# ScalarE's order inside one head of two softmax attentions: all four exponentials, then the copies

## The chip, the cores and the metric

The kernel is one program on one core of a Trainium2 chip. The metric is the device time of one execution in microseconds (us), the median over several. One core has five engines that run independently and meet only at semaphores: TensorE (PE, with its weight loads as PEld), VectorE (DVE), ScalarE (ACT), GpSimd (POOL) and SyncE (SP, which issues transfers). Each works through its own list of instructions in order.

## The reference

Two model blocks run one after the other on 512 positions of width 1024. Two attentions in the second block matter here: a sparse one with 8 heads of width 64, in which each query sees at most 128 chosen keys, and a latent one with 16 heads of width 64 + 32.

```python
# layer 0: 8 heads, keys chosen per query (here a mask added to the logits does the choosing)
logits = jnp.einsum('bqhd,bqkhd->bhqk', qb, k_sel).astype(jnp.float32) * (dh ** -0.5)
logits = jnp.where(valid[:, None], logits, -jnp.inf)
p = jax.nn.softmax(logits, axis=-1).astype(v.dtype)
return jnp.einsum('bhqk,bqkhd->bqhd', p, v_sel).reshape(bsz, Q_BLOCK, h * dh)
...
# layer 1: 16 heads, causal
logits = (jnp.einsum('bqhd,bshd->bhqs', qnb, k_nope)
          + jnp.einsum('bqhr,bsr->bhqs', qrb, k_rope)).astype(jnp.float32) * scale
p = jax.nn.softmax(logits, axis=-1).astype(v.dtype)
return jnp.einsum('bhqs,bshd->bqhd', p, v).reshape(bsz, Q_BLOCK, C_HEADS * C_V_DIM)
```

Each of them is followed by an output product, norms and a squared-ReLU MLP.

## The kernel before

A head has four blocks of 128 queries. Query block t sees 128(t+1) keys, so one head has logits of 512, 384, 128 and 256 columns for t = 3, 2, 0, 1. They lie in three banks of PSUM. Even heads use the tile PM, odd heads the tile PDT (PX[n % 2] in the code), so two heads are in the works at once. The last bank (index 3) of each tile serves other products.

A head n passes through the engines like this:

1. TensorE, `logits(n)` (L1558): eight groups of products for the four query blocks, written to PX[n % 2]. Ahead of them it waits in `probs_taken` for both copies of head n-2, which lay in the same banks.
2. VectorE, `row_least(n)` (L3162): adds the mask, takes the least of each row (the logits carry a minus sign), and raises att_max once for each of the four blocks.
3. ScalarE, `exps(n)` (L2297): four exponentials, each followed by a read of the row sum.
4. TensorE, `turn_probs(n)` (L1576): ten 128x128 transposes, back into the same banks. It waits for all four exponentials.
5. ScalarE, `turned(n)` (L2304), copies the first bank (512 columns) of the turned probabilities out, and VectorE, also `turned(n)` (L3169), the other two (768 columns). Only then are the banks free for head n+2.
6. TensorE, `pair_values` (L1597): the products with the values, for two heads together, in two halves; every second head also turns the row sums (`turn_den`, L1584).

The loops are software-pipelined by hand. In step h TensorE does logits(h), then (latent attention only) `turn_q(h + 2)` (L1684), which turns the query of a later head, then turn_probs(h-1), then values. In step h ScalarE does exps(h) and turned(h-1), in the latent attention also `turned_q(h + 2)` (L2369), a copy of the turned query. TensorE's wait is

```python
def probs_taken(n):
    pe.wait_ge(S("probs_s"), n)
    pe.wait_ge(S("probs_v"), n)
```

where probs_s is raised by ScalarE's copy and probs_v by VectorE's; logits(h) is preceded by probs_taken(h-1), that is by the copies of head h-2. `turn_q(h + 2)` waits for tr_read, which ScalarE raises with turned_q(h+1): all turned queries from head 1 on pass through one bank, PDT bank 3.

Of the kernel before, what the change touches and what calls it, by code (L numbers as in the profile page):

```python
# [51 lines left out]
A_H = 8  # L52
TOPK = 128
C_H = 16
# [113 lines left out]
def build_program(nc, x, c, w_ada, b_ada, norm_in_gain, w_in, conv_w, conv_b, dt_bias, a_log, d_skip,  # L168
# [15 lines left out]
    def S(name):  # L184
        if name not in sems:
            sems[name] = ctx.enter_context(nc.semaphore(name))
        return sems[name]
# [60 lines left out]
    def arena(name, shape, kb, dtype=F32):  # L248
        return at(name, shape, dtype, offset=A0 + int(kb * KB))
# [66 lines left out]
    pr = [arena("pr0", [P, 1280], 8), arena("pr1", [P, 1280], 13)]  # L316
# [3 lines left out]
    mx = arena("mx", [P, 4, TT], 77.625)  # L320
    den = arena("den", [P, 4, TT], 77.75)
# [29 lines left out]
    pr3 = [arena("pr30", [P, 1280], 9), arena("pr31", [P, 1280], 16)]  # L351
# [4 lines left out]
    mx3 = arena("mx3", [P, 4, TT], 26)  # L356
    den3 = arena("den3", [P, 4, TT], 26.5)
# [95 lines left out]
    def full_wait(eng, name, b, r, unit):  # L453

        if b < 3:
            eng.wait_ge(S(f"bank_full{b}"), r + (PH[name][2][b] + 1))
        else:
            eng.wait_ge(S("w_used"), unit + 1)
# [61 lines left out]
    def head_group(h):  # L520

        return TR["heads"][0] + 1 + h + max(0, (h - 4) // 2)
# [1233 lines left out]
    def _(act):  # L1756
# [363 lines left out]
        def after_piece(name, r, h, b):  # L2120

            u = PH[name][0] + 2 * r + h
            if (b == last_bank(name, r, h) or name == "dt") and (name, r, h) not in (("wout_a", 1, 1), ("z_attn", 0, 1), ("qk2", 1, 1),
                                                               ("gates", 2, 1)):
                hi(0, u + 2, 0)
            if h == 1 and name != "z_attn":
                full_wait(act, name, b, r, u)
                if name == "gates":
                    dst = gb[:, b, :]
                elif name == "xbc":  # L2130
                    dst = xbc[:, 4 * r + b, 3:SEQ + 3]
                else:
                    dst = {"z_ssm": zs, "wout_a": mix, "qk2": qk_tm}[name][:, b, 512 * r:512 * r + 512]
                scale = rstd[:, 1, b:b + 1] if name == "wout_a" else 1.0
                nc.scalar.activation(dst, PD[b], ACT.Copy, scale=scale).then_inc(S(f"bank_free{b}"), 1)
# [145 lines left out]
        def convolution2_high(f):  # L2281
            act.wait_ge(S("w_used"), PH["wo2"][0])
            act.wait_ge(S("conv2_out"), f + 1)
            nc.scalar.activation(hhi[:, 4 + f, :], ca[:, f, :], ACT.Copy).then_inc(S("conv2_hi"), 1)

        def exps(n, p, m, d, order):

            s = n % 2
            if n >= 2:
                act.wait_ge(S("att_turned"), n - 1)  # L2290
            if n >= 4:
                act.wait_ge(S("den_wide"), n - 3)
            for q, t in order:
                b, c0 = QB_AT[t]
                w = (t + 1) * P
                act.wait_ge(S("att_max"), 4 * n + (1, 3, 3, 4)[q])
                nc.scalar.activation(p[s][:, QB_FIRST[t]:QB_FIRST[t] + w], PX[s][:, b, c0:c0 + w], ACT.Exp, scale=-1.0,  # L2297
                                     bias=m[:, n % 4, t:t + 1], accum_out=d[:, n % 4, t:t + 1]).then_inc(S("att_exps"), 1)

        def turned(n, pt):  # L2300
            act.wait_ge(S("att_turned"), n + 1)
            if n >= 4:
                act.wait_ge(S("att_pv"), n // 2 - 1)
            nc.scalar.activation(pt[n % 4][:, 0:SEQ], PX[n % 2][:, 0, :], ACT.Copy).then_inc(S("probs_s"), 1)  # L2304

        def turned_den(pair):

            act.wait_ge(S("tr_done"), den_group(pair) + 1)
            if pair >= 2:
                act.wait_ge(S("attn_low"), KT + pair - 1)  # L2310
            nc.scalar.activation(lat[pair % 2][:, :], den_bank(pair), ACT.Copy).then_inc(S("tr_read"), 1)

        def lat_high(pair, k):

            act.wait_ge(S("att_out"), pair + 1)
            nc.scalar.activation(hhi[:, k, :], lat[pair % 2][:, :], ACT.Copy).then_inc(S("attn_high"), 1)

        for h in range(A_H + 4):
            if h < A_H:
                exps(h, pr, mx, den, ((0, 3), (1, 2)))  # L2320
            if 1 <= h <= A_H:
                turned(h - 1, prt)
            if h < A_H:
                exps(h, pr, mx, den, ((2, 0), (3, 1)))
            if h == 2:
                after_piece(*GATE_PIECES[7])
            if 3 <= h < 7:
                convolution2_high(h - 3)
            if h >= 5 and h % 2:
                lat_high((h - 5) // 2, (h - 5) // 2)  # L2330
            if h >= 3 and h % 2 and h < A_H + 3:
                turned_den((h - 3) // 2)
# [33 lines left out]
        def turned_q(h):  # L2366
            act.wait_ge(S("tr_done"), head_group(h) + 1)
            X = PDT if h else PM
            nc.scalar.activation(qth[h % 2][0:C_QK, :], X[0:C_QK, 3, :], ACT.Copy, scale=-C_QK ** -0.5)\  # L2369
                .then_inc(S("tr_read"), 1)  # L2370
# [23 lines left out]
        for h in range(C_H + 4):  # L2394
            n = A_H + h
            if h < C_H:
                exps(n, pr3, mx3, den3, ((0, 3), (1, 2)))
            if h + 2 < C_H:
                turned_q(h + 2)
            if h == 3:  # L2400
                act.wait_ge(S("w_used"), PH["wo3"][0])
            if 1 <= h <= C_H:
                turned(n - 1, prt3)
            if h < C_H:
                exps(n, pr3, mx3, den3, ((2, 0), (3, 1)))
            if h in (1, 2):
                full_wait(act, "ukv", h + 1, 3, u0 + 1)
                nc.scalar.activation(v3[:, h + 1, 512:DM], PM[:, 3, :], ACT.Copy).then_inc(S(f"bank_free{h + 1}"), 1)
            if h >= 5 and h % 2:
                lat_high((n - 5) // 2, (h - 5) // 2)  # L2410
            if h >= 3 and h % 2 and h < C_H + 3:
                turned_den((n - 3) // 2)
# [180 lines left out]
    def _(dve):  # L2593
# [776 lines left out]
        def ends(name):  # L3370
# [13 lines left out]
            def fifth(_):  # L3384

                m = mixm[:, 2:4, 512:DM]
                v.tensor_tensor(m, m, PDT[:, 2:4, :], ALU.subtract).then_inc(S("mlp_sum"), 1)

            def seventh(_):

                dve.wait_ge(S("w_used"), u + turn_of(3, P7) + 1)
                dve.wait_ge(S("mlp_sum"), made + 7)
                m = mixm[:, 2:4, 512:DM]
                v.tensor_tensor(m, m, PDT[:, 0:2, :], ALU.subtract).then_inc(S("mlp_sum"), 1)
                m = mixm[:, 2:4, 0:512]
                v.tensor_tensor(m, m, PDT[:, 0:2, :], ALU.add).then_inc(S("mlp_sum"), 1)

            def last_lo(_):

                dve.wait_ge(S("w_hi"), u + P4 + 1)  # L3400
                raw, w = wraw[RAW[u + P4][0]], (u + P4) % 2
                v.tensor_tensor(wlo[w][:, :], raw[:, :], fl(whi[w][:, :]), ALU.subtract).then_inc(S("w_split"), 1)
# [91 lines left out]
```

## Time and profile before

| | |
|---|---|
| median of 3 runs | 1733.22 us |
| lowest and highest | 1733.17, 1734.76 us |
| the profiled execution | 1732.95 us, of which the span of the profile 1731.1 us |
| granted TensorE clock, mean over the span | 0.998 |
| busy share of the span | PE 98%, DVE 63%, ACT 52%, POOL 22% |
| the sparse attention (8 heads) | about 759 to 795 us in the span |
| the latent attention (16 heads) | about 1256 to 1343 us in the span |

A row of a timeline has the start in us, the duration in us, the engine, the line, the operation, output<-inputs, the sizes, and how many instructions it merges; in brackets the idle time of the engine ahead of it and what ended that. A duration beside neighbours that start before it has ended is normal: instructions of one engine overlap a little.

### The profile page before, as it was taken

What the parts mean: (1) busy time and instruction counts of PE and PEld (TensorE: products, weight loads), DVE (VectorE), ACT (ScalarE), POOL (GpSimd) and SP (SyncE); (2) the same over time, 40 slices, a digit from 0 to 9 for tenths busy, and PEclk for the clock granted to TensorE, in tenths of its full rate; (3) what the DMA queues carried; (4) which work ended last, traced back from release to release, by engine and by line L of the source; (5) the groups of instructions that cost most, each with busy time, mean ns of one, the idle gap of its engine ahead of it and who ended that gap; (6) DMA issues with size and microseconds to landing.
All of it is one profiled execution on the core that took longest, in us unless ns stands there. A gap on an engine that the chain in (4) does not pass through costs nothing.

```text
span 1731.1 us, 21441 instructions
## 1 busy us (share of the span) xinstructions
PE 1695.2 (98%) x8391; PEld 1364.7 (79%) x8391; DVE 1097.2 (63%) x1449; ACT 896.7 (52%) x1428; POOL 377.2 (22%) x226
## 2 busy tenths in 40 slices
PE   7999999999999999999999999998999999999997
PEld 5898777778787867877988888888866798888886
DVE  6786567685976367953455565595457246565488
ACT  4435656556635353255564535456677356353553
POOL 0200232123244233433400100105410340010100
PEclk9999999999999999999999999999999999999999
DMA  8632322222132322223377775782310247775695
GB/s 318 231 121 75 97 63 65 71 73 72 51 122 81 98 73 72 96 77 110 108 182 187 161 199 145 171 192 83 104 60 1 97 153 164 195 157 184 146 218 135
DMA packets 109377, 216.62 MB, mean 125 GB/s; under 512 B 6905, under 2 KB 9086, under 8 KB 109278
## 3 DMA queue, kind: packets, MB, share of 16 engines
q1 hardware_dynamic: 89214, 175.42, 30.8%
q0 software_dynamic: 20064, 39.85, 13.7%
q8 instruction: 66, 1.08, 0.3%
q14 instruction: 33, 0.27, 0.0%
HBM read 205.88 MB, written 2.10 MB: 120 GB/s over the span
## 4 chain that ended last, share of the span: by engine, by line
PE 88%; DVE 7%; ACT 2%; issue 2%; DMA 1%; POOL 0%; SPq 0%; DVEq 0%; ACTq 0%
PE PDT L873 9%; PE PDT L875 9%; PE PDT L874 9%; PE PDT L862 6%; PE PDT L864 6%; PE PDT L863 6%; PE PM L1070 5%; PE PM L1063 5%; PE PM L1065 5%; PE PM L1321 2%; PE PM L1597 2%; PE PM L1288 1%; PE PM L1558 1%; PE PDT L1558 1%; PE PM L1349 1%
## 5 line engine op out<-in xcount | busy, mean ns | idle before, releaser
L2442 POOL TENSOR_TENSOR wlo<-wraw,whi 128x512 fp32r<-128x512 f32 (+5 forms) x103 | 284.4, 2779 | 570.0 <-ACT whi L1771 398.6
L3217 DVE TENSOR_TENSOR wlo<-wraw,whi 128x2048 fp32r<-128x2048 f32 x82 | 187.9, 2292 | 197.1 <-ACT whi L1889 196.9
L1889 ACT ACTIVATE whi<-wraw 128x2048 fp32r<-128x2048 f32 x82 | 157.1, 1916 | 260.8 <-PE PM L1070 131.8
L873 PE MATMUL PDT<-hhi,whi 128*128 128x512 f32 x732 | 287.4, 393 | 1.1 <-POOL wlo L2442 1.1
L875 PE MATMUL PDT<-hhi,wlo 128*128 128x512 f32 x732 | 285.2, 390 | 0.0
L874 PE MATMUL PDT<-hlo,whi 128*128 128x512 f32 x732 | 285.2, 390 | 0.0
L862 PE MATMUL PDT<-whi,hhi 128*128 128x512 f32 (+1 forms) x528 | 208.0, 394 | 1.1 <-DVE hlo L2951 0.6
L864 PE MATMUL PDT<-whi,hlo 128*128 128x512 f32 (+1 forms) x528 | 202.9, 384 | 0.0
L863 PE MATMUL PDT<-wlo,hhi 128*128 128x512 f32 (+1 forms) x528 | 202.9, 384 | 0.0
L1771 ACT ACTIVATE whi<-wraw 128x2048 fp32r<-128x2048 f32 (+4 forms) x63 | 113.9, 1808 | 131.4 <-PE PDT L864 59.9
L2568 POOL DMA_DIRECT2D wraw<-in_mlp_w x38 | 49.4, 1301 | 541.7 <-DMA wraw<-in_mlp_w 488.0
L873 PEld LDWEIGHTS PDT<-hhi,whi 128*128 128x128 f32 x732 | 137.5, 188 | 29.6 <-POOL wlo L2442 1.5
L875 PEld LDWEIGHTS PDT<-hhi,wlo 128*128 128x128 f32 x732 | 137.4, 188 | 28.9
L874 PEld LDWEIGHTS PDT<-hlo,whi 128*128 128x128 f32 x732 | 137.5, 188 | 27.5
L1063 PE MATMUL PM<-whi,part_hi 128*128 128x512 f32 x352 | 136.9, 389 | 0.0
L1065 PE MATMUL PM<-whi,part_lo 128*128 128x512 f32 x352 | 136.9, 389 | 0.0
L862 PEld LDWEIGHTS PDT<-whi,hhi 128*128 128x128 f32 x528 | 99.1, 188 | 34.2 <-issue 14.8
L864 PEld LDWEIGHTS PDT<-whi,hlo 128*128 128x128 f32 x528 | 99.1, 188 | 20.0
L863 PEld LDWEIGHTS PDT<-wlo,hhi 128*128 128x128 f32 x528 | 99.2, 188 | 18.8 <-issue 0.7
L1070 PE MATMUL PM<-wlo,part_hi 128*128 128x512 f32 x352 | 86.9, 389 | 0.0
L3258 DVE TENSOR_TENSOR mixm<-mixm,PM 128x1024 f32<-128x1024 f32 x50 | 60.4, 1218 | 33.1 <-PE PM L1070 33.1
L1063 PEld LDWEIGHTS PM<-whi,part_hi 128*128 128x128 f32 x352 | 66.1, 188 | 13.7
(469 smaller groups left out, 3165.0 us busy)
## 6 DMA issues: line engine op xcount, KB each, us to landing
wraw<-in_mlp_w SPq DMA_DIRECT2D x72, 1024.0 KB, 5.3
wraw<-in_mlp_w POOLq DMA_DIRECT2D x38, 1024.0 KB, 8.9
wraw<-in_w_in SPq DMA_DIRECT2D x22, 1024.0 KB, 5.2
wraw<-in_even_w_in SPq DMA_DIRECT2D x16, 1024.0 KB, 5.2
w_ada<-in_w_ada SPq DMA_DIRECT2D x11, 1024.0 KB, 13.2
wraw<-in_w_out SPq DMA_DIRECT2D x8, 1024.0 KB, 5.0
kv_raw<-in_w_in SPq DMA_DIRECT2D x4, 1024.0 KB, 7.3
swapped<-qk_sb SPq DMA_DIRECT2D x16, 256.0 KB, 6.6
```

The costliest lines, as they stand in the source:

```text
L862: mm(bank, sth, wh[:, k, c0:c0 + n], start=start and k == 0, stop=False)
L863: mm(bank, sth, wl[:, k, c0:c0 + n], start=False, stop=False)
L864: last = mm(bank, stl, wh[:, k, c0:c0 + n], start=False, stop=stop and k == kn - 1)
L873: mm(bank, sth, hi[:, k0 + k, :], start=start and k == 0, stop=False)
L874: mm(bank, sth, lo[:, k0 + k, :], start=False, stop=False)
L875: last = mm(bank, stl, hi[:, k0 + k, :], start=False, stop=stop and k == 3)
L1063: mm(banks[t], part_hi[n][:, k, rows], wh[:, k, :], start=start and k == 0, stop=False, skip_group_check=True)
L1065: mm(banks[t], part_lo[n][:, k, rows], wh[:, k, :], start=False, stop=False, skip_group_check=True)
L1070: last = mm(banks[t], part_hi[n][:, k, t * P:t * P + P], wl[:, k, :], start=False, stop=k == 3, skip_group_check=True)
L1889: nc.scalar.activation(whi[u % 2][:, :], wraw[slot][:, :], ACT.Copy).then_inc(S("w_hi"), 1)
L2442: part = g.tensor_tensor(wlo[base % 2][:, cols], wraw[base % 2][:, cols], fl(whi[base % 2][:, cols]), ALU.subtract)
L3217: v.tensor_tensor(wlo[u % 2][:, :], raw[:, :], fl(whi[u % 2][:, :]), ALU.subtract).then_inc(S("w_split"), 1)
```

## The change

On ScalarE, `exps` makes its four exponentials (t = 3, 2, 0, 1) in one go. Before, the last two stood behind the copy of turned probabilities (sparse attention), or behind the copy of a turned query and then that of turned probabilities (latent attention). Now these copies stand behind all four; in the latent attention the probabilities' copy now comes ahead of the query's.

```diff
         for h in range(A_H + 4):
             if h < A_H:
-                exps(h, pr, mx, den, ((0, 3), (1, 2)))
+                exps(h, pr, mx, den, ((0, 3), (1, 2), (2, 0), (3, 1)))
             if 1 <= h <= A_H:
                 turned(h - 1, prt)
-            if h < A_H:
-                exps(h, pr, mx, den, ((2, 0), (3, 1)))
             if h == 2:
                 after_piece(*GATE_PIECES[7])
...
             if h < C_H:
-                exps(n, pr3, mx3, den3, ((0, 3), (1, 2)))
-            if h + 2 < C_H:
-                turned_q(h + 2)
+                exps(n, pr3, mx3, den3, ((0, 3), (1, 2), (2, 0), (3, 1)))
             if h == 3:
                 act.wait_ge(S("w_used"), PH["wo3"][0])
             if 1 <= h <= C_H:
                 turned(n - 1, prt3)
-            if h < C_H:
-                exps(n, pr3, mx3, den3, ((2, 0), (3, 1)))
+            if h + 2 < C_H:
+                turned_q(h + 2)
```

The other four engines keep their lists unchanged. On ScalarE, the sparse attention at heads 2 and 3 (pr are the exponentials, prt the turned probabilities, the numbers are buffers) becomes:

```order
-L2304 ACTIVATE prt_152<-PDT 128x512
 L2297 ACTIVATE pr_149,den<-PM,mx 128x128
 L2297 ACTIVATE pr_149,den<-PM,mx 128x256
+L2304 ACTIVATE prt_152<-PDT 128x512
 L2135 ACTIVATE gb<-PDT 128x512
 L2297 ACTIVATE pr_150,den<-PDT,mx 128x512
 L2297 ACTIVATE pr_150,den<-PDT,mx 128x384
-L2304 ACTIVATE prt_153<-PM 128x512
 L2297 ACTIVATE pr_150,den<-PDT,mx 128x128
 L2297 ACTIVATE pr_150,den<-PDT,mx 128x256
+L2304 ACTIVATE prt_153<-PM 128x512
```

The copy of each head has moved behind two exponentials, and behind nothing else.

At the start of the latent attention ScalarE had this order before (qth is a turned query, L2408 a copy of values):

```order
L2297 ACTIVATE pr_217,den_226<-PM,mx_225 128x512
L2297 ACTIVATE pr_217,den_226<-PM,mx_225 128x384
L2369 ACTIVATE qth_215<-PDT 96x512
L2297 ACTIVATE pr_217,den_226<-PM,mx_225 128x128
L2297 ACTIVATE pr_217,den_226<-PM,mx_225 128x256
L2297 ACTIVATE pr_218,den_226<-PDT,mx_225 128x512
L2297 ACTIVATE pr_218,den_226<-PDT,mx_225 128x384
L2369 ACTIVATE qth_216<-PDT 96x512
L2304 ACTIVATE prt_219<-PM 128x512
L2297 ACTIVATE pr_218,den_226<-PDT,mx_225 128x128
L2297 ACTIVATE pr_218,den_226<-PDT,mx_225 128x256
L2408 ACTIVATE v_213<-PM 128x512
```

and has this one now (its lines from there on are numbered up to four lower):

```order
L2297 ACTIVATE pr_217,den_226<-PM,mx_225 128x512
L2297 ACTIVATE pr_217,den_226<-PM,mx_225 128x384
L2297 ACTIVATE pr_217,den_226<-PM,mx_225 128x128
L2297 ACTIVATE pr_217,den_226<-PM,mx_225 128x256
L2367 ACTIVATE qth_215<-PDT 96x512
L2297 ACTIVATE pr_218,den_226<-PDT,mx_225 128x512
L2297 ACTIVATE pr_218,den_226<-PDT,mx_225 128x384
L2297 ACTIVATE pr_218,den_226<-PDT,mx_225 128x128
L2297 ACTIVATE pr_218,den_226<-PDT,mx_225 128x256
L2304 ACTIVATE prt_219<-PM 128x512
L2367 ACTIVATE qth_216<-PDT 96x512
L2404 ACTIVATE v_213<-PM 128x512
```

The first query's copy stands behind two more exponentials. From the second step on the probabilities' copy stands behind two more exponentials but ahead of the query's copy, which stands last.

## Rows read from the trace of the kernel before

**Rows 1.** The page: span, TensorE's busy time, the last chain by engine.
```profile
span 1731.1 us, 21441 instructions
PE 1695.2 (98%) x8391; PEld 1364.7 (79%) x8391; DVE 1097.2 (63%) x1449; ACT 896.7 (52%) x1428; POOL 377.2 (22%) x226
PE 88%; DVE 7%; ACT 2%; issue 2%; DMA 1%; POOL 0%; SPq 0%; DVEq 0%; ACTq 0%
```

**Rows 2.** Windows: busy us (instructions) of PE, PEld, DVE, ACT, POOL; clock; DMA.
```profile
759.00:795.00 36.00, 33.58 (x217) 22.16 (x216) 25.15 (x85) 26.81 (x83) 13.85 (x16) 1.00 0.26 71
1256.00:1343.00 87.00, 86.27 (x513) 58.85 (x513) 56.37 (x171) 63.15 (x180) 10.55 (x16) 1.00 0.09 28
```

**Rows 3.** Timeline of PE, sparse attention.
```profile
766.22 0.66 PE L1558 MATMUL PM<-qkt 64*128 64x512 f32 x1 [0.40 <-ACT prt L2304]
...
770.22 0.66 PE L1558 MATMUL PDT<-qkt 64*128 64x512 f32 x1 [0.52 <-DVE prt L3169]
...
774.51 0.69 PE L1558 MATMUL PM<-qkt 64*128 64x512 f32 x1
...
787.17 0.69 PE L1558 MATMUL PDT<-qkt 64*128 64x512 f32 x1
...
788.66 1.31 PE L1576 MATMUL PM<-ident,pr 128*128 128x128 f32 x10
...
790.91 0.66 PE L1584 MATMUL PDT<-ident,den_wide 128*128 128x128 f32 x4
791.91 1.31 PE L1576 MATMUL PDT<-ident,pr 128*128 128x128 f32 x10 [0.34 <-ACT pr L2297]
```

**Rows 4.** Timeline of DVE, sparse attention.
```profile
769.12 0.95 DVE L3169 COPY prt<-PDT 128x768 f32<-128x768 f32 x1
...
771.35 0.70 DVE L3162 CUSTOM_DVE_ANT_0 PDT<-PDT,bias_q 128x512 f32<-128x512 f32 x1 [1.19 <-PE PDT L1558]
```

**Rows 5.** Timeline of ACT, sparse attention, step 3 and one later copy.
```profile
772.20 0.69 ACT L2297 ACTIVATE pr<-PDT,mx 128x512 f32<-128x512 f32 x1 [0.84 <-DVE mx L3162]
...
773.47 0.59 ACT L2304 ACTIVATE prt<-PM 128x512 f32<-128x512 f32 x1
773.95 0.37 ACT L2297 ACTIVATE pr<-PDT,mx 128x128 f32<-128x128 f32 x1
...
774.29 0.48 ACT L2297 ACTIVATE pr<-PDT,mx 128x256 f32<-128x256 f32 x1
...
774.74 0.65 ACT L2284 ACTIVATE hhi<-ca 128x512 fp32r<-128x512 f32 x1
...
786.29 0.59 ACT L2304 ACTIVATE prt<-PDT 128x512 f32<-128x512 f32 x1
```

**Rows 6.** Timelines of ACT and PEld: from a ScalarE copy to TensorE.
```profile
758.29 1.08 ACT L1803 ACTIVATE qkt<-PM 128x512 f32<-128x512 f32 x2
...
759.42 0.18 PEld L1558 LDWEIGHTS PM<-qkt 64*128 64x128 f32 x1 [0.53 <-ACT qkt L1803]
```

**Rows 7.** Timelines of ACT and PE, start of the latent attention.
```profile
1263.71 0.59 ACT L2369 ACTIVATE qth<-PDT 96x512 f32<-96x512 f32 x1
...
1264.53 0.48 ACT L2297 ACTIVATE pr<-PM,mx 128x256 f32<-128x256 f32 x1
...
1264.97 0.69 ACT L2297 ACTIVATE pr<-PDT,mx 128x512 f32<-128x512 f32 x1
...
1264.76 0.60 PE L1684 MATMUL PDT<-ident,q_tm 128*96 128x128 f32 x4
```

**Rows 8.** Timelines of ACT and PE, latent attention, a middle and the last copy.
```profile
1303.18 0.60 ACT L2304 ACTIVATE prt<-PDT 128x512 f32<-128x512 f32 x1
...
1304.51 2.42 PE L1558 MATMUL PDT<-kt,qth 96*128 96x512 f32 x8
...
1334.61 0.60 ACT L2304 ACTIVATE prt<-PDT 128x512 f32<-128x512 f32 x1
...
1335.94 2.43 PE L1558 MATMUL PDT<-kt,qth 96*128 96x512 f32 x8
```

## The prediction

> **What bounds the kernel now.** I read the page first: TensorE is busy for 98% of the span, and the chain that ended last lies on it for 88% and on ScalarE for 2% [rows 1]. So a move on ScalarE matters only where TensorE waits for it, and only two stretches are touched. The windows show that TensorE is busy for 33.58 of 36.00 us in the sparse attention, and for 86.27 of 87.00 in the latent one [rows 2]. The most that the change could give back is the difference, 2.4 and 0.7 us, and only if all of that were due to late exponentials. Then I read the timelines of TensorE for these gaps. Of those charged to ScalarE's exponentials, one can be touched: 0.34 us ahead of the last transposes of the sparse attention [rows 3]. (The transposes of head 0 wait too, but nothing stood between its exponentials before.) Two more, 0.40 and 0.52 us, stand ahead of the logits of heads 2 and 3 [rows 3]: there TensorE waits for the copies of turned probabilities, which are what the change makes later. In the middle of the sparse attention TensorE has no gap ahead of the logits: from head 2 to head 7 they start at 766.22 to 787.17, a mean of 4.19 us a head [rows 3].
>
> **How much later the copies come.** ScalarE does the same work in both orders, so only positions matter. Two exponentials with their row sums take from 773.95 to the next start at 774.74, 0.79 us [rows 5]. In the sparse attention each copy of probabilities is 0.79 us later behind its head's first exponential. In the latent attention it also drops the query's copy from ahead of it. That copy lasts 0.59, and from start to start I take 0.48, as for the equally wide probabilities' copy (773.47 to 773.95 [rows 5]); so the copy is 0.79 - 0.48 = 0.31 us later.
>
> **Sparse attention.** What decides is a loop: logits of head h, VectorE's first row minimum, ScalarE's exponentials of head h, the copy of head h-1, logits of head h+1. I add it up from rows:
>
> - logits start to VectorE's start: 770.22 to 771.35, 1.13 us [rows 3, 4];
> - VectorE's start to the first exponential: 771.35 to 772.20, 0.85 [rows 4, 5]; other heads show up to 0.88 and I take 0.86;
> - first exponential to the copy's start: 772.20 to 773.47, 1.27 [rows 5], now with 0.79 added: 2.06;
> - the copy 0.59 [rows 5], and from its end to TensorE 0.05 to 0.06: the copies of 758.29 end at 759.37 and the weight load starts at 759.42 [rows 6].
>
> Before, that makes 3.90 us, less than TensorE's own 4.19 a head, so the copy was hidden by 0.3 to 0.5 us. Now it makes 1.13 + 0.86 + 2.06 + 0.59 + 0.06 = 4.70 us, and TensorE has to wait in each step. The mean step grows by 4.70 - 4.19 = 0.51. Head 2 is delayed by about 0.1 first (an estimate: ScalarE's copy, which ended 0.46 ahead of those logits, moves by about 0.5 and ends just behind VectorE's, with the shorter release). Over the five steps from head 2 to head 7 this gives 5 x 0.51 + 0.1 = 2.65 us at the logits of head 7.
>
> A part is returned at the end. The transposes of head 7 waited 0.34 for exponentials that stood behind a copy. Now the last exponential is 0.48 earlier counted from its own logits. TensorE's queue of head 7 then decides: 788.66 - 787.17 = 1.49 for the logits, 790.91 - 788.66 = 2.25 for transposes and values, about 0.58 for the turned sums (their 0.66, less the overlap with what follows), together 4.32, against 791.91 - 787.17 = 4.74 before [rows 3]: 0.42 back. The sparse attention ends 2.65 - 0.42 = **2.2 us later**. If the release took 0.15 us, as it does from VectorE's copy (769.12 + 0.95 = 770.07 to 770.22 [rows 3, 4]), the loop would be 4.80 and the sum 2.8.
>
> **Latent attention, steady steps.** The copy at 1303.18 ends at 1303.78, and the logits that need it start at 1304.51, 0.73 us later [rows 8]. The even heads have 0.8. Shifting the copy by 0.31 leaves 0.42. In the sparse attention a copy that ends at 786.88 released logits at 787.17 with no gap [rows 3, 5], so 0.29 is enough, and the 12 or so steady heads cost nothing. The query's copy, now last, is about 1.3 us later, but its reader turn_q comes only behind the next head's logits (2.16 us), so it too is covered. What is covered here would cost about 0.3 a head if the cover were gone. The last pair of heads has no query copy to drop: the copy at 1334.61 moves by up to 0.79 and ends at about 1335.94, just when the logits used to start [rows 8]: 0.05 to 0.15 us.
>
> **Latent attention, start.** Step 0 has no probabilities' copy, so the query copy of head 2 is purely later: from 1263.71 to about 1264.50, ending at 1265.09 [rows 7]. The transposes of head 3's query start at 1264.76 [rows 7] and need that bank. They now wait until about 1265.15: **0.4 us**. ScalarE loses nothing, the exponential of 1264.97 [rows 7] starts when it did. Nothing behind in that attention has room to win it back, since TensorE has only 0.7 us of gaps in 87, most of them ahead of this point.
>
> **What else could move.** POOL's and VectorE's reciprocals get the row sums earlier; nobody waits for them. Transfers are held by semaphores that TensorE's progress raises, so they move with it. The copy of row sums on ScalarE in the last steps of the sparse attention moves with the loop and keeps over 1 us to its reader.
>
> **Sum.** 2.2 + 0.1 + 0.4 = 2.7 us, on the profiled execution's 1732.95: 1735.65. The median of the runs shown is 0.27 higher, so I forecast 1735.9 us, 0.16% slower. About 0.2% (3.5 us) is what a measurement of this kernel can tell from no change, so this counts as within it, close to its edge.
>
> **Rivals.**
>
> - *Copies late in the latent attention too* (slower by over 0.2%). If the 0.42 us left there are not enough, because TensorE's queue wants the semaphore before the last values' products are issued, each of 12 to 14 heads pays. It decides from 0.06 us a head on: 13 x 0.06 = 0.8, which with 2.7 passes 3.5. At 0.2 a head the time is 1735.9 + 2.6 = 1738.5. Against it speaks the pair with 0.29. The milder form is the 0.15 us release in the sparse attention: 2.8 + 0.6 = 3.4, 1736.6, right at the edge. Together 0.22.
> - *TensorE's clock drops in the sparse attention.* It now stands about 0.4 to 0.5 us in each of five heads. The rows show a clock of 1.00 there with two such gaps already [rows 2, 3]. If the five steps of 4.19 us ran at 1.2 in place of 2.4 GHz, their work would at most double: up to +21 us, 1757. Against it: such gaps are few and TensorE stays over 85% busy. 0.02. The Trainium skill, "TensorE: Matmul & The Clock Gate", section "A second HAM failure mode: psum-queue depth-cycling", tells of short idles between groups of matmuls that made the clock swing between its levels. By that rule this change would be costly; the gaps of 0.40 and 0.52 at a clock of 1.00 speak against it here.
> - *The waits are absorbed.* The kernel loses nothing: either TensorE's gaps close later in a place that waits on something not moved (the norms and MLP after the sparse attention), or the copy's lateness is hidden. Time 1733.2 to 1734.0. For it speaks only that there are a few gaps later; against it, that they hang on TensorE's own results. 0.08.
> - *Earlier exponentials win.* The transposes wait less. Only 0.34 us of that kind of wait is there to be removed, so the gain alone is 0.3, 1732.9. To pass 0.2% the change would need gaps that the rows don't show. 0.03 for faster, and 0.65 for my forecast.
>
> **How the numbers follow.** The range runs from 1733.7 (most of the waits absorbed) to 1737.5 (the longer release, and 0.06 us a head in the latent attention); 0.8 lies in it. My own case alone spans 1735.2 to 1736.7. Faster by over 0.2%: 0.03. Slower by over 0.2%: 0.22 from the first rival, 0.02 from the clock and 0.02 from my own case's upper tail, 0.26. Within: 0.71.
>
> **What would show it.** In the profile after: in the sparse attention, logits (L1558) of heads 3 to 7 with an idle time of 0.3 to 0.9 us each ahead of them, ended by ScalarE's prt (L2304), and starts 4.7 us apart; no idle time ahead of the last transposes; the first output product (L862) 2.2 us later than before. In the latent attention, one gap of about 0.4 ahead of the second or third L1684, ended by qth, and no gaps ahead of L1558 but the last, with copies ending about 0.4 ahead of the logits. The span between the two attentions unchanged in length. I am wrong if the steps stay near 4.2 us, if gaps stand in each latent head, or if the clock in the first window is below 1.00.

## The result: slower by 0.37%, and the profile after

The changed kernel took 1739.51 us (median of 6 runs, 1739.26 to 1741.15) against 1733.14 for the kernel before, measured beside it. The ratio is 1.0037 with a 95% interval of 1.0027 to 1.0048. The forecast was 1735.9 in a range to 1737.5.

The page of the kernel after begins with its span and the busy times, as in [rows 1]:

```profile
span 1739.0 us, 21419 instructions
...
PE 1698.0 (98%) x8391; PEld 1366.6 (79%) x8391; DVE 1097.7 (63%) x1449; ACT 897.0 (52%) x1428; POOL 377.3 (22%) x226
```

ScalarE does the same work in the same time, so the 6.4 us are not more work on it. Windows over the two attentions of the kernel after (columns as in [rows 2]; the second starts 4 us ahead of the first logits as the window of before does, the first starts 2.1 us ahead of them, where that of before starts 0.4 ahead):

```profile
759.00:797.00 38.00, 33.41 (x218) 22.71 (x216) 23.40 (x81) 26.97 (x84) 13.23 (x15) 1.00 0.17 50
...
1260.00:1351.00 91.00, 86.75 (x513) 58.85 (x513) 56.94 (x171) 63.29 (x180) 10.57 (x16) 1.00 0.08 27
```

The clock is still 1.00 in both. TensorE stands idle for 4.6 us in the first window and 4.3 in the second, against 2.4 and 0.7. To compare kernels I measure each attention from the start of its first logits (L1558) to the start of the first output product (L862). Between exactly these ends TensorE is idle for 4.49 us in place of 2.33 in the sparse attention, and for 3.51 in place of none in the latent one. The stretch between the attentions (465.4 us) and the one behind them (387.5) kept their lengths; the profiled execution of after also lost 1.7 us ahead of the first attention, where nothing was changed, so its span is longer than the medians' difference says.

| stretch, us | before | after | difference |
|---|---|---|---|
| sparse attention | 794.59 - 759.42 = 35.17 | 798.59 - 761.08 = 37.51 | +2.34 |
| latent attention | 1343.63 - 1259.99 = 83.64 | 1351.55 - 1264.00 = 87.55 | +3.91 |

**Sparse attention.** The timeline of TensorE in the kernel after, to be read beside [rows 3]:

```profile
768.00 0.69 PE L1558 MATMUL PM<-qkt 64*128 64x512 f32 x1 [0.51 <-ACT prt L2304]
...
772.74 0.69 PE L1558 MATMUL PDT<-qkt 64*128 64x512 f32 x1 [1.24 <-ACT prt L2304]
...
777.47 0.69 PE L1558 MATMUL PM<-qkt 64*128 64x512 f32 x1 [0.33 <-ACT prt L2304]
...
791.67 0.69 PE L1558 MATMUL PDT<-qkt 64*128 64x512 f32 x1 [0.50 <-ACT prt L2304]
...
795.91 1.31 PE L1576 MATMUL PDT<-ident,pr 128*128 128x128 f32 x10
...
798.59 0.50 PE L862 MATMUL PDT<-whi,hhi 128*128 128x512 f32 x1
```

Every logits from head 2 on waits for ScalarE's copy, and the five steps from 768.00 to 791.67 take 4.73 us each (4.70 forecast, 4.19 before). The wait is what TensorE's own work leaves of the 4.73: ahead of head 3 it is 1.24, more than the 0.9 that I had named as the most, because that step took 4.00 us before, of which 0.52 were already a wait [rows 3]. The wait of 0.34 ahead of the last transposes is gone. ScalarE's own timeline shows the copy behind the exponentials of 128 and 256 columns:

```profile
774.75 0.69 ACT L2297 ACTIVATE pr<-PDT,mx 128x512 f32<-128x512 f32 x1 [1.58 <-DVE mx L3158]
...
776.02 0.36 ACT L2297 ACTIVATE pr<-PDT,mx 128x128 f32<-128x128 f32 x1
...
776.81 0.60 ACT L2304 ACTIVATE prt<-PM 128x512 f32<-128x512 f32 x1
```

It starts 2.06 behind the first exponential, as worked out, and ends at 777.41, 0.06 ahead of the logits of 777.47.

**Latent attention.** TensorE in the kernel after, steps 1, 3 and 15:

```profile
1269.15 0.64 PE L1684 MATMUL PDT<-ident,q_tm 128*96 128x128 f32 x4 [0.23 <-ACT qth L2367]
...
1280.98 1.08 PE L1597 MATMUL PM<-prt,v 128*64 128x384 f32 x8
1282.62 0.63 PE L1584 MATMUL PDT<-ident,den_wide 128*128 128x128 f32 x4 [0.55 <-POOL den_wide L2526]
1283.08 2.32 PE L1558 MATMUL PM<-kt,qth 96*128 96x512 f32 x8
...
1343.97 2.43 PE L1558 MATMUL PDT<-kt,qth 96*128 96x512 f32 x8
```

The first line is the forecast stall at the start: it shows 0.23 us as idle time, and the transposes start 0.38 us later behind the first logits than before (1269.15 - 1264.00 = 5.15 in place of 4.77). The one ahead of L1584, the turning of row sums, was not forecast. It stands in steps 3, 5, 7, 9, 11 and 13; in step 15, where no query is turned any more, L1584 starts without a wait. The row charges it to GpSimd's widened sums. GpSimd's timeline in the same kernel speaks against that:

```profile
1277.11 0.40 POOL L2526 COPY den_wide<-den 128x256 f32<-128x256 f32 x1 [4.68 <-DVE den L3171]
1282.20 0.40 POOL L2526 COPY den_wide<-den 128x256 f32<-128x256 f32 x1 [4.68 <-DVE den L3171]
```

L1584 of step 3 turns the sums of heads 0 and 1, and head 1's were widened by 1277.51, five microseconds before. The row of 1282.20 is head 2's and is needed by nobody yet; its end, 1282.60, only happens to be the last event. What else ends there is ScalarE's copy of the turned query:

```profile
1281.40 0.60 ACT L2304 ACTIVATE prt<-PM 128x512 f32<-128x512 f32 x1
...
1281.88 0.59 ACT L2367 ACTIVATE qth<-PDT 96x512 f32<-96x512 f32 x1
```

It ends at 1282.47. Turned row sums go through the same bank as turned queries (`den_bank` gives PDT bank 3, `turn_q` writes PDT[..., 3, :]), and `turn_den` waits for tr_read in the same step: `pe.wait_ge(S("tr_read"), den_group(pair))`. That is the theory of the shared bank. The rivals: GpSimd, as the row says; or the probabilities' copies, late here too.

### The profile page after: what moved, and what is told of

The parts are those of the page before. It is cut to its first block, busy times and chain, and to the rows that moved or that the text cites. A ratio compares the mean times of both kernels' runs of the same rounds, so it can differ in the third digit from the quotient of the medians.

```text
span 1739.0 us, 21419 instructions
## 1 busy us (share of the span) xinstructions
PE 1698.0 (98%) x8391; PEld 1366.6 (79%) x8391; DVE 1097.7 (63%) x1449; ACT 897.0 (52%) x1428; POOL 377.3 (22%) x226
## 4 chain that ended last, share of the span: by engine, by line
PE 81%; DVE 7%; issue 6%; ACT 3%; POOL 1%; DMA 1%; SPq 0%; DVEq 0%; POOLq 0%; ACTq 0%
PE PDT L873 9%; PE PDT L875 9%; PE PDT L874 9%; PE PDT L862 6%; PE PDT L864 6%; PE PDT L863 6%; PE PM L1070 5%; PE PM L1063 5%; PE PM L1065 5%; PE PM L1321 2%; PE PM L1288 1%; PE PM L1349 1%; PE PM L1524 1%; PE PDT L1003 1%; PE PDT L1008 1%
## 5 line engine op out<-in xcount | busy, mean ns | idle before, releaser
L862 PE MATMUL PDT<-whi,hhi 128*128 128x512 f32 (+1 forms) x528 | 208.0, 394 | 1.1 <-DVE hlo L2947 0.6
L862 PEld LDWEIGHTS PDT<-whi,hhi 128*128 128x128 f32 x528 | 99.1, 188 | 34.3 <-issue 14.8
L1065 PEld LDWEIGHTS PM<-whi,part_lo 128*128 128x128 f32 x352 | 66.1, 188 | 13.7
```

The source lines that it names most:

```text
L862: mm(bank, sth, wh[:, k, c0:c0 + n], start=start and k == 0, stop=False)
L1065: mm(banks[t], part_lo[n][:, k, rows], wh[:, k, :], start=False, stop=False, skip_group_check=True)
```

## The experiments

Each run is compared with runs of the kernel before on its own chip. "Latent" is the length measured as above, with 83.64 as the value of before.

| run | median, us | before beside it | ratio and 95% interval | latent, us |
|---|---|---|---|---|
| e1_sparse_only | 1735.51 | 1733.16 | 1.0017 (1.0008 to 1.0026) | 83.64 |
| e2_latent_only | 1737.0 | 1733.16 | 1.0023 (1.0013 to 1.0033) | 87.53 |
| e4_query_copy_last | 1739.99 | 1733.16 | 1.0046 (1.0032 to 1.0059) | 90.58 |
| e8_even_steps_only | 1733.54 | 1733.16 | 1.0002 (0.9993 to 1.0012) | 84.11 |
| e5_widen_twice | 1740.1 | 1733.17 | 1.0042 (1.0025 to 1.0059) | 87.51 |
| e3_query_stays | 1736.44 | 1733.17 | 1.0014 (1.0004 to 1.0024) | 85.79 |
| e6_query_then_probs | 1735.88 | 1733.17 | 1.0012 (1.0002 to 1.0022) | 85.74 |
| e7_sparse_last_head | 1732.85 | 1733.17 | 0.9998 (0.9988 to 1.0007) | 83.64 |

### The two halves apart

e1 applies only the first hunk of the change and e2 only the second.

> The new order in the sparse attention alone. Both theories of the latent attention say the same here: the loop of logits, exponentials and copy sets the step at 4.73 us in place of 4.2, which the profile after showed as 2.3 us from the first logits to the first output product (37.5 in place of 35.2 us). So 1735.5 us beside 1733.1. If the 6.4 us were one effect of both halves together, this would be under 1 us.

> The new order in the latent attention alone. Theory (shared bank): turning the row sums (L1584) needs PDT bank 3, which the late copy of the turned query still holds; 0.59 us in each of six odd steps and 0.4 in step 1, 3.9 us, so 1737.0. Rival (my forecast's own reading): only 0.4 to 0.6 us here and the rest is from elsewhere, so 1733.7.

e1 measured 1735.51, and its sparse attention took 37.52 us. e2 measured 1737.0, with 87.53 in the latent attention and 35.17 in the sparse one. Each half lengthens its own attention by what the whole change does (37.51 and 87.55) and leaves the other as it was. The ratios less one, 0.17% and 0.23%, add up to 0.40% against 0.37% for both, which agrees within intervals of about 0.1%. So the halves are independent, and more than half of the loss is in the latent attention, where 0.5 us had been forecast.

### Is it GpSimd? The sums widened twice

The changed kernel, with

```diff
+            if n >= A_H:
+                g.tensor_copy(wide[pair % 2][:, :, c0:c0 + HD], d[:, n % 4, :].unsqueeze(2).to_broadcast([P, TT, HD]))\
+                    .then_inc(S("widened_once"), 1)
+                pool.wait_ge(S("widened_once"), n - A_H + 1)
             g.tensor_copy(wide[pair % 2][:, :, c0:c0 + HD], d[:, n % 4, :].unsqueeze(2).to_broadcast([P, TT, HD]))\
                 .then_inc(S("den_wide"), 1)
```

> Changed kernel, with GpSimd widening each latent head's row sums twice, one after the other (about 0.45 us more a head). Shared bank: L1584 needs the sums of a head whose widening ended 5 us before, so no change beside the changed kernel, 1739.4, waits of 0.55 ahead of L1584 as before. Rival (GpSimd, as the row names it): the wait becomes 1.0, six times 0.45 more, 1742.

The latent attention takes 87.51 us, as in the changed kernel (87.55), where the rival asked for 2.7 more. The median of 1740.1 alone would not decide: 1742 is a ratio of 1.0051, inside the interval of four timings. The timelines of ScalarE, GpSimd and TensorE around step 3:

```profile
1280.20 0.59 ACT L2367 ACTIVATE qth<-PDT 96x512 f32<-96x512 f32 x1
...
1280.53 0.40 POOL L2527 COPY den_wide<-den 128x256 f32<-128x256 f32 x1 [4.21 <-DVE den L3175]
...
1280.94 0.63 PE L1584 MATMUL PDT<-ident,den_wide 128*128 128x128 f32 x4 [0.54 <-ACT qth L2367]
1280.99 0.40 POOL L2530 COPY den_wide<-den 128x256 f32<-128x256 f32 x1
```

TensorE turns the sums while GpSimd has the second widening of head 2 still to do. With the coincidence gone, all six rows now name the query's copy, at 0.54 to 0.55 us as before. GpSimd is ruled out.

### The query's copy alone

The kernel before, with the query's copy at the end of the step; the exponentials stay in two pairs around the probabilities' copy.

```diff
                 exps(n, pr3, mx3, den3, ((0, 3), (1, 2)))
-            if h + 2 < C_H:
-                turned_q(h + 2)
...
                 exps(n, pr3, mx3, den3, ((2, 0), (3, 1)))
+            if h + 2 < C_H:
+                turned_q(h + 2)
```

> Kernel before, but in the latent attention the query's copy alone is moved to the end of the step; the other two exponentials stay behind the copy of probabilities, which comes 0.5 us earlier. Shared bank: the query's copy ends when it does in the changed kernel, so the same 0.55 us wait stands ahead of each L1584 of steps 3 to 13, 3.9 us in all, 1737.0. Rival (GpSimd's widened sums are what L1584 waits for, as the row of the profile says, because of the order of exponentials): sums are read when they were before, so no wait, 1733.1. Rival (copies of probabilities late): these are earlier, so 1733.1.

The waits ahead of L1584 appear with nothing but that copy moved, and they are charged to it. But they are 1.09 us in step 3 and 1.04 in the other five, not 0.55, and the run is 3 us slower than I expected, slower than the changed kernel in its latent half. TensorE in step 3, and ScalarE in step 4:

```profile
1279.22 0.63 PE L1584 MATMUL PDT<-ident,den_wide 128*128 128x128 f32 x4 [1.09 <-ACT qth L2369]
...
1283.57 0.60 ACT L2304 ACTIVATE prt<-PDT 128x512 f32<-128x512 f32 x1 [0.39 <-PE PDT L1576]
```

I had taken the probabilities' copy to move 0.5 us forward. It can't: it waits for the transposes (L1576), so ScalarE idles about 0.4 us in each step and everything behind it, the query's copy last, is late by that too. Six waits of about 1.05 and the 0.4 at the start are 6.7 us, and the stage grew by 6.94. In the order of before, the query's copy filled this hole.

### Only the steps without row sums

TensorE turns row sums in odd steps. Here the new order holds in even steps, the old one in odd steps.

```diff
-                exps(n, pr3, mx3, den3, ((0, 3), (1, 2)))
-            if h + 2 < C_H:
+                exps(n, pr3, mx3, den3, ((0, 3), (1, 2)) if h % 2 else ((0, 3), (1, 2), (2, 0), (3, 1)))
+            if h + 2 < C_H and h % 2:
                 turned_q(h + 2)
...
-            if h < C_H:
+            if h < C_H and h % 2:
                 exps(n, pr3, mx3, den3, ((2, 0), (3, 1)))
+            if h + 2 < C_H and h % 2 == 0:
+                turned_q(h + 2)
```

> Latent attention, new order in even steps only; odd steps, in which TensorE turns row sums (L1584), keep the old order. Shared bank: no wait ahead of L1584, and only the 0.38 us of step 1 ahead of L1684 and at most 0.05 a step at the logits are left: 1733.5 to 1733.9. Rival (probabilities' copies late by 0.31): half of the heads would still pay, some 2 us, 1735.

1733.54, a ratio of 1.0002. The latent attention takes 84.11 us, 0.47 more than before, of which the start's stall is the most. TensorE in steps 1 and 3:

```profile
1265.24 0.64 PE L1684 MATMUL PDT<-ident,q_tm 128*96 128x128 f32 x4 [0.23 <-ACT qth L2369]
...
1277.06 1.08 PE L1597 MATMUL PM<-prt,v 128*64 128x384 f32 x8
1278.07 0.66 PE L1584 MATMUL PDT<-ident,den_wide 128*128 128x128 f32 x4
```

No wait ahead of L1584. The probabilities' copy, 0.31 us later in the even steps, costs next to nothing, as forecast. (That is so for the odd heads' copies, which fall in even steps.) So 3.4 of the 3.9 us stand and fall with the order in the odd steps, and e4 shows that of this order the query's place alone is enough to bring the waits.

### The query's copy kept early, the probabilities' copy 0.79 later

In e3 the four exponentials come ahead of the probabilities' copy, with the query's copy in its old place (behind the second); in e6 the query's copy follows the fourth exponential, and the probabilities' copy comes last. e3:

```diff
                 exps(n, pr3, mx3, den3, ((0, 3), (1, 2)))
             if h + 2 < C_H:
                 turned_q(h + 2)
+            if h < C_H:
+                exps(n, pr3, mx3, den3, ((2, 0), (3, 1)))
...
                 turned(n - 1, prt3)
-            if h < C_H:
-                exps(n, pr3, mx3, den3, ((2, 0), (3, 1)))
```

e6:

```diff
-                exps(n, pr3, mx3, den3, ((0, 3), (1, 2)))
+                exps(n, pr3, mx3, den3, ((0, 3), (1, 2), (2, 0), (3, 1)))
             if h + 2 < C_H:
                 turned_q(h + 2)
...
                 turned(n - 1, prt3)
-            if h < C_H:
-                exps(n, pr3, mx3, den3, ((2, 0), (3, 1)))
```

> Kernel before, but in the latent attention all four exponentials ahead of the probabilities' copy while the query's copy stays behind the second exponential. The probabilities' copy is then 0.79 us later than before, against 0.73 (odd heads) and 0.80 (even) of room. Shared bank: no waits at L1584 and L1684; small waits at the logits, 0.05 to 0.15 a head, 1 us in all, 1734.2. Rival (order of exponentials or GpSimd makes L1584 late): 0.55 a pair stays, 1737.

> Kernel before, but in the latent attention all four exponentials, then the query's copy, then the probabilities'. The query's copy is 0.48 earlier than in the changed kernel, so the shared bank leaves a wait of 0.55 - 0.48 = 0.1 ahead of L1584; 0.38 stays in step 1; the probabilities' copy is 0.79 later than before and costs about 0.1 at every second logits. Together about 1.9 us, 1735.0. Rival (GpSimd): 0.55 stays, 1737 or more.

In both no wait is charged at L1584. In e3 the logits pay instead. In e6 L1584 of the steps from 3 on starts 2.77 us behind L1684 (1275.08 to 1277.85) where it was 2.64 before: that is the 0.13 us expected there, though no row shows it as idle time, and the logits pay about as much again. e3's head 2, of TensorE:

```profile
1268.29 2.43 PE L1558 MATMUL PM<-kt,qth 96*128 96x512 f32 x8 [0.29 <-ACT prt L2304]
```

e6 grew by 2.10 us in the stage (1.9 expected). e3 grew by 2.15, twice what I had expected: 0.9 us of it is in the first four steps, and each later pair of heads costs 0.23 (10.85 us a pair against 10.62, from the starts of even heads' logits). I had counted the room from a copy's end to the logits' start as free to the last 0.06 us; from head 4 on the logits start on time to within 0.1, but those of the even heads run 2.43 in place of 2.32 (the odd heads' ran 2.43 before, too). e3's median is 3.3 above before where its stage explains 2.15. Its profiled execution was its slowest of the ten, and the stretch behind the latent attention is 3.3 us longer in it (390.8 in place of 387.5). Two waits stand there, in the last MLP, far from the change:

```profile
1703.25 0.47 PE L1063 MATMUL PM<-whi,part_hi 128*128 128x512 f32 x1 [0.76 <-ACT whi L1889]
...
1712.23 1.19 PE L1070 MATMUL PDT<-wlo,part_hi 128*128 128x512 f32 x4 [1.47 <-DVE wlo L3217]
```

No other trace here shows these waits. Whether e3's order makes it likelier or it is scatter, its ten timings (1734.92 to 1738.49) don't tell.

### The last head of the sparse attention alone

```diff
-                exps(h, pr, mx, den, ((0, 3), (1, 2)))
+                exps(h, pr, mx, den, ((0, 3), (1, 2)) if h < A_H - 1 else ((0, 3), (1, 2), (2, 0), (3, 1)))
...
-            if h < A_H:
+            if h < A_H - 1:
                 exps(h, pr, mx, den, ((2, 0), (3, 1)))
```

> Kernel before, new order for the last head of the sparse attention alone, where no logits follow the copy. The wait of 0.34 us ahead of the last L1576 is gone, and nothing else moves: 0.4 us faster in the profile, 1732.7, which the timing can't tell from no change. Rival: the copy of row sums and the last copies come later and a wait of like size opens ahead of the first L862: no gain.

The last transposes start with no wait, and the attention takes 34.68 us in place of 35.17:

```profile
791.54 1.31 PE L1576 MATMUL PDT<-ident,pr 128*128 128x128 f32 x10
```

The stretch up to the latent attention is 465.72 against 465.40, so 0.3 of the 0.5 us is given back there. The timing shows no change (0.9998). This is the only part of the change for which a trace shows a gain, and none of the versions tried beats the kernel before by more than can be measured.

## Why the prediction was wrong

**Sparse attention: right.** The loop of logits, row minimum, exponentials and copy was forecast at 4.70 us and measured at 4.73. The logits of head 7 come 2.84 us late (2.65 forecast), and 0.50 is returned at the end (0.42 forecast: the 0.58 taken for the turned sums is 0.50, 795.41 to 795.91). The two misses partly cancel: the sum was +2.2 and measured +2.34, and e1 confirms it alone.

**Latent attention, probabilities' copies: right.** 0.31 us later with 0.42 left was enough (e8, for the odd heads; the even heads' copies, with 0.8 us of room, were moved without the waits at L1584 only in e3 and e6, by 0.79). The margin is smaller than I took it for, though: at 0.79 later, e3 pays 2.15 us and e6 about 0.9 of its 2.10 (the start takes 0.4 and L1584 six times 0.13).

**Latent attention, start: right.** 0.4 forecast; the transposes of head 3's query start 0.38 later against the first logits than before. The last pair's 0.1 shows as 0.07 at the logits of head 15 and is gone again at the first output product.

**The step that failed** is this one of the prediction: "The query's copy, now last, is about 1.3 us later, but its reader turn_q comes only behind the next head's logits (2.16 us), so it too is covered." The bank that this copy frees has two writers, turn_q and turn_den. I followed only the first. The second comes in the same step, directly behind half of the values. In step 3 of the kernel before, ScalarE and TensorE:

```profile
1276.16 0.58 ACT L2369 ACTIVATE qth<-PDT 96x512 f32<-96x512 f32 x1
...
1277.56 0.66 PE L1584 MATMUL PDT<-ident,den_wide 128*128 128x128 f32 x4
1278.05 2.32 PE L1558 MATMUL PM<-kt,qth 96*128 96x512 f32 x8
```

The query's copy ended at 1276.74, 0.82 us ahead of L1584. Against its step's logits it now comes 1.28 us later (1281.88 - 1277.20 = 4.68 in place of 1276.16 - 1272.76 = 3.40), which is too late by 0.46, and TensorE starts 0.15 behind its end: 0.6 us. It returns six times: 6 x 0.59 = 3.5 us (the pairs' starts are 11.21 apart in place of 10.62). 2.2 + 0.5 + 3.5 = 6.2, beside the measured 6.4.

**The rivals.** "Copies late in the latent attention too" named the right attention and about the right price (1738.5), but the wrong copy and the wrong waiter; that the price was near is luck. The clock did not fall, though TensorE stood 0.33 to 1.24 us ahead of the logits of each head from 2 on: it is 1.00 in the window of the profile after. By the rule of the Trainium skill, "TensorE: Matmul & The Clock Gate", section "A second HAM failure mode: psum-queue depth-cycling", which the prediction names, it might have swung; this kernel's trace doesn't show it. Nothing was absorbed, and earlier exponentials gave 0.5 us at the most.

## What to carry to other kernels

When a copy out of a shared buffer is moved, list everything that writes the buffer next, by the counter that the copy raises and not by the tensor's name: each engine that waits for that counter depends on the order. In a hand-made pipeline a copy between two others may be there as a filler for a wait; taking it out leaves the hole and moves the copy into somebody's way. And where a wait's releaser is charged to an engine whose product was long ready, doubling that engine's work is a cheap test of the charge.

## What I had not expected of the hardware

TensorE started 0.06 us after the end of ScalarE's copy of probabilities (777.41 to 777.47), but 0.15 after the end of its copy of the query (1282.47 to 1282.62, and 1280.79 to 1280.94 in e5). Why this is so was not tried. A late copy need not show as idle time of TensorE at all: in e3 the logits of the even heads from 4 on have no idle time charged to them, but run 2.43 us in place of 2.32.
